# RWKV-7 steps of a two-layer hybrid diffusion backbone: key products, decay preparation and transposes put at other places in the step

## The reference

```python
def step(S, inp):
    r_t, w_t, k_t, v_t, kk_t, a_t = inp
    sa = jnp.einsum('bhij,bhj->bhi', S, kk_t)
    S = (S * w_t[:, :, None, :] - sa[..., None] * (kk_t * a_t)[:, :, None, :]
         + v_t[..., None] * k_t[:, :, None, :])
    return S, jnp.einsum('bhij,bhj->bhi', S, r_t)
```

## Time and profile before

| | |
|---|---|
| runs (3) | median 2116.42 us, 2113.2 to 2116.71 |
| the profiled execution | 2119.79 us, its span 2117.8 us |
| busy share of the span | PE 94%, PEld 87%, DVE 62%, ACT 42%, POOL 36% |
| RWKV steps | about 387 to 553 us (layer 0) and 1425 to 1595 us (layer 1) |
| granted TensorE clock, mean of the span | 0.975 |

### The profile page before, as it was taken

How to read it: one execution, slowest core, us unless ns; L and a number is a source line. 1 busy time by engine, 2 the same in 40 slices (tenths; PEclk the granted TensorE clock), 3 DMA queues, 4 the chain that set the end, 5 groups by cost and what they waited for, 6 DMA issues and landing times.

```text
span 2117.8 us, 47803 instructions
## 1 busy us (share of the span) xinstructions
PE 1980.8 (94%) x20520; PEld 1836.1 (87%) x20520; DVE 1304.2 (62%) x2049; ACT 895.8 (42%) x1701; POOL 769.2 (36%) x603
## 2 busy tenths in 40 slices
PE   6999999888999999999979999988889989999998
PEld 5998866677898999999979987657778989999998
DVE  5755347566679888831239452675566898888112
ACT  4535554333445444531154364544343544445221
POOL 5332244333433434332213321742252334343431
PEclk8999999899999999999989999999999999999999
DMA  8553210000122332344225432000001222232221
GB/s 271 162 169 120 78 19 2 22 28 3 47 77 60 94 86 80 88 140 140 83 90 180 149 109 61 9 22 3 28 25 51 70 77 84 80 91 78 75 80 67
DMA packets 255272, 169.42 MB, mean 80 GB/s; under 512 B 23873, under 2 KB 228223, under 8 KB 255063
## 3 DMA queue, kind: packets, MB, share of 16 engines
q1 hardware_dynamic: 254835, 166.32, 26.1%
q10 hardware_dynamic: 227, 0.07, 0.0%
HBM read 162.21 MB, written 4.15 MB: 79 GB/s over the span
## 4 chain that ended last, share of the span: by engine, by line
PE 77%; DVE 11%; ACT 7%; issue 2%; SPq 1%; POOL 1%; DMA 1%; DVEq 0%; ACTq 0%; POOLq 0%
PE PS L1126 12%; PE PS L1128 12%; PE PS L1127 12%; PE PS L1809 7%; PE PS L1810 7%; PE PS L1811 7%; PE PS L1537 5%; PE PS L1084 2%; ACT arena L2177 1%; SPq L542 1%; PE PS L1559 1%; DVE U_r L3195 1%; DVE U L2806 1%; ACT whi_r L2006 1%; PE PS L1192 1%
## 5 line engine op out<-in xcount | busy, mean ns | idle before, releaser
L781 POOL TENSOR_TENSOR ring_r<-ring,whi_r 128x1024 fp32r<-128x1024 f32 (+1 forms) x128 | 311.3, 2433 | 685.4 <-ACT whi_r L2006 685.4
L1126 PE MATMUL PS<-rwp_r,whi_r 128*128 128x320 f32 x1440 | 455.7, 316 | 12.4 <-DVE arena_r L2468 4.6
L1128 PE MATMUL PS<-rwp_r,ring_r 128*128 128x320 f32 x1440 | 448.0, 311 | 0.0
L1127 PE MATMUL PS<-U_r,whi_r 128*128 128x320 f32 (+1 forms) x1048 | 323.9, 309 | 0.0
L1126 PEld LDWEIGHTS PS<-rwp_r,whi_r 128*128 128x128 f32 x1440 | 273.3, 190 | 26.5 <-issue 19.5
L1127 PE MATMUL PS<-arena_r,whi_r 128*128 128x320 f32 (+1 forms) x904 | 282.3, 312 | 0.0
L1128 PEld LDWEIGHTS PS<-rwp_r,ring_r 128*128 128x128 f32 x1440 | 273.2, 190 | 0.0
L2006 ACT ACTIVATE whi_r<-ring 128x1024 fp32r<-128x1024 f32 (+1 forms) x128 | 131.2, 1027 | 296.1 <-PE PS L1128 295.2
L1127 PEld LDWEIGHTS PS<-U_r,whi_r 128*128 128x128 f32 x1048 | 196.9, 188 | 0.3
L2464 DVE TENSOR_TENSOR arena<-arena 128x640 f32<-128x640 f32 x32 | 61.2, 1912 | 214.8 <-ACT arena L1945 214.4
L1127 PEld LDWEIGHTS PS<-arena_r,whi_r 128*128 128x128 f32 x904 | 172.8, 191 | 0.2
(11 more groups left out here) (506 smaller groups left out, 4956.1 us busy)
## 6 DMA issues: line engine op xcount, KB each, us to landing
ring<-in_ffn_w SPq DMA_DIRECT2D x120, 512.0 KB, 3.8
rwp<-in_ada_w SPq DMA_DIRECT2D x64, 512.0 KB, 4.8
ring<-in_w_in SPq DMA_DIRECT2D x50, 512.0 KB, 4.6
U<-in_ada_w SPq DMA_DIRECT2D x16, 512.0 KB, 9.2
ring<-in_w_out SPq DMA_DIRECT2D x16, 512.0 KB, 3.8
arena<-in_ada_w SPq DMA_DIRECT2D x16, 512.0 KB, 4.6
ring<-in_ffn_w SPq DMA_DIRECT2D x16, 384.0 KB, 3.2
out<-arena SPq DMA_DIRECT2D x5, 512.0 KB, 3.6
```

Source lines behind the costliest of these rows:

```text
L781: g.tensor_tensor(rings_r[:, slot_of[n], 0:size(n), :], slot(n)[:, 0:size(n), :], whis[:, q % 2, 0:size(n), :].bitcast(F32), ALU.subtract) ...
L1126: mm(out, w[0][:, k, :], hi[:, cols], start=start, stop=False)
L1127: mm(out, w[0][:, k, :], lo[:, cols], start=False, stop=False)
L1128: return mm(out, w[1][:, k, :], hi[:, cols], start=False, stop=stop)
```

## The change

Four edits, all inside the RWKV steps. No instruction is added or taken away; five places in the lists and one wait are moved.
- PE: the key products (L1559) stand ahead of the first round of the doubling in steps 1, 3 and 4. Steps 0 and 2 keep the old order.
- PE: the wait for `yr_read` stands ahead of the diagonal products, not ahead of the transposes.
- DVE: `prep_scan(k + 1)` is split by unit. Unit `l` is prepared at the head of level `l`, ahead of its adds; and `adds(2, 3)` stands ahead of the mask of the feature products (L2932).
- ACT: `decays(k + 1)` is split by unit. Unit `l` stands behind the copies of level `l`.

```diff
@@ PE
                             pe.wait_ge(s["rw_keys"], at["rw_keys"] + i + 1)
-                            if k:
-                                pe.wait_ge(s["yr_read"], at["yr_read"] + i - 1)
...
                             pe.wait_ge(s["rw_feat"], at["rw_feat"] + i + 1)
+                            if k:
+                                pe.wait_ge(s["yr_read"], at["yr_read"] + i - 1)
...
+                        if k in (0, 2):
+                            first_round()
+                            key_products()
+                        else:
+                            key_products()
+                            first_round()
@@ ACT
-                        if k < NC - 1:
-                            decays(k + 1)
-                        else:
+                        if k == NC - 1:
                             y_high(range(3, 4))
...
                         for l in range(2):
                             copies(3 + l, 4 + 2 * l)
+                            if k < NC - 1:
+                                decays(k + 1, l)
@@ DVE
                         adds(0, 1)
-                        if k < NC - 1:
-                            prep_scan(k + 1)
-                        else:
+                        if k == NC - 1:
...
                         adds(1, 2)
+                        adds(2, 3)
                         for d in range(2):
...
-                        adds(2, 3)
                         if k == 3:
                             ssd_scaled([3])
                         for l in range(2):
+                            if k < NC - 1:
+                                prep_scan(k + 1, (l,))
                             adds(3 + l, 5 + 2 * l)
```

More of the change, by code:

```diff
@@ L1545, in added, with first_round @@
                             pe.wait_ge(s["inv_add"], at["inv_add"] + 10 * k + 2 * r + d + 1)
[L1547 to L1561, removed]
+                        def first_round():
+                            for d in range(2):
+                                pe.wait_ge(s["rw_q"], at["rw_q"] + 2 * k + d + 1)
+                                each(d, 2, 0, "QT", "Q")
+                                each(d, 2, 256, "Q", "QT").then_inc(s["inv_mm"], 1)
@@ new lines, in key_products @@
+                        def key_products():
+                            for d in range(2):
+                                b, a, i = units[d], 4 * d, 2 * k + d
+                                pe.wait_ge(s["rw_tok"], at["rw_tok"] + 2 * i + 2)
+                                if i == 0:
+                                    pe.wait_ge(s["yn_read"], at["yn_read"] + 1)
+                                if i == 4:
+                                    pe.wait_ge(s["yn_read"], at["yn_read"] + 2)
+                                for hh, (f, q) in enumerate(hq):
+                                    ins = mm(PS[:, a + hh % 2, 256 * f:256 * f + 256],
+                                             b["KB"][q, f, 0, :], b["RK"][k % 2][q, f, :, :], start=True, stop=True)
+                                ins.then_inc(s["rw_prod"], 1)
@@ L2189, in y_high, with decays @@
                             A(rp_r[:, YSEQ[n], :], U[:, YTILES[YSEQ[n]], :], ACT.Copy).then_inc(s["in_hi"], 1)
[L2191 to L2206, removed]
+                    def decays(k, d):
+                        b, i = units[d], 2 * k + d
+                        act.wait_ge(s["rs_dve"], at["rs_dve"] + i + 1)
+                        if k:
+                            act.wait_ge(s["rw_feat"], at["rw_feat"] + i - 1)
+                            act.wait_ge(s["rw_last"], at["rw_last"] + i - 1)
+                            if k > 1:
+                                act.wait_ge(s["sp_ready"], at["sp_ready"] + i - 3)
+                        A(b["e2"], b["c"], ACT.Exp, scale=ISQE)
+                        A(b["e1"], b["c"], ACT.Exp, scale=-ISQE)
+                        A(b["e3"], b["e3"], ACT.Exp, scale=-ISQE)
+                        A(EMID[:, 2 * d:2 * d + 2], MID[:, 2 * d:2 * d + 2], ACT.Exp, scale=-ISQE).then_inc(s["rs_exp"], 1)
+                    for d in range(2):
+                        decays(0, d)
                     for c in range(NC - 2, NC):
@@ L2792, in mlstm_centre, with prep_scan @@
                         dve.wait_ge(s["dve_step"], step())
-                    def prep_scan(k):
-                        for d in range(2):
+                    def prep_scan(k, ds):
+                        for d in ds:
                             b, i = units[d], 2 * k + d
@@ L2836, in _ @@
                         else:
-                            prep_scan(0)
+                            prep_scan(0, range(2))
                         normalise(c)
```

## The result

| | median us | lowest to highest | runs |
|---|---|---|---|
| before | 2115.78 | 2113.2 to 2116.71 | 4 |
| after | 2095.32 | 2092.18 to 2097.18 | 4 |

The ratio is 0.9899, with a 95% interval of 0.9884 to 0.9914: 20.5 us less between the medians. The forecast was 2088.3 us with a range of 2079 to 2101. The profiled execution of after took 2094.3 us, its span 2092.3 us, at a mean granted clock of 0.978.

What follows compares the result with a forecast made beforehand. PE was taken to bound the kernel (77% of the chain), so gains come where it waits. Steps 26.0, contention -2.4 and clock +4.5 gave 28.1 us off 2116.42: 2088.3 us, range 2079 to 2101.

Steps and rivals of the forecast that it cites:

- Key products: PE's list, steps 1, 3 and 4: key products ahead of the first round start the second round 2.0 us earlier.
- Preparation and early sum: DVE, around fourth round and first level: removed waits gain 1.5 + 0.6, less 0.75 given back: 1.35 us a step.
- 0.75 us given back: Second level: unit 0's preparation delays the first level's sum, so PE starts that level 0.7 to 0.75 us later.
- Transposes: Start of steps 2, 3 and 4: no wait for DVE's read, gaining 1.0, 0.35 and 1.0 us.
- ACT's new place: ACT, inside the levels: unit 0's decays take 1.1 us ahead of a copy, hidden by 0.5 us; unit 1's use idle time.
- Step 4: Inside step 4, without preparation: ACT's splits limit the first level's copies to 2.1 us earlier, counted as the whole inside gain.
- Contention in steps 2 and 3: DVE's unit 1 preparation and row scalings beside POOL's keys: 0.6 us lost in each step, 2.4 in two layers.
- Clock: RWKV steps: five low-clock stretches behind PE's removed waits become two, gaining 3 x 1.5 = 4.5 us.
- Its own range: Main case's range, 2080 to 2094 us: one clock stretch more or less, contention from 0 to 4 us.
- Contention at its upper bound: Rival, chance 0.12: DVE beside POOL's keys loses 6.4 us a layer, clock gives only 1.5; time 2101.7 us.

Runs made afterwards that it cites:

- e1: Kernel before with only the key products moved ahead of the first round in steps 1, 3 and 4: 2101.27 us, ratio 0.9930.
- e2: Kernel after with PE's part as before, so only the preparation, decays and adds(2, 3) are moved: 2109.88 us, ratio 0.9968.
- e5: Kernel after with step 4's key products behind the first round again: 2092.05 us, ratio 0.9883.
- e8: Kernel after with unit 0 prepared behind adds(0, 1), unit 1 ahead of the second level's sums, step 2's row scalings put apart: 2091.38 us, ratio 0.9873.
- e3: Kernel before with only the wait for yr_read moved from the transposes to the diagonal products: 2110.82 us, ratio 0.9968.
- e7: Kernel after, with POOL's keys from step 1 on waiting until DVE has prepared both units: 2088.24 us, ratio 0.9870.
- e9: Kernel after with step 4's gating held, POOL's keys held until preparation ends, and unit 0 prepared early: 2077.93 us, ratio 0.9810.
- e11: Kernel before with key products first in steps 1, 3 and 4, and POOL's gating held in step 4: 2095.17 us, ratio 0.9889.
- e10: Kernel before with only POOL's gating in step 4 held until DVE's two products are done: 2113.76 us, ratio 0.9981.
- e6: Kernel after, with POOL's gating in step 4 held until DVE's two products are done: 2088.39 us, ratio 0.9857.

## Why the prediction was right, and where it was not

The time fell within the range, 7.0 us above the forecast: 20.5 us gained where 28.1 were forecast, with a median of before that one more run took from 2116.42 to 2115.78. By its own steps:

- **Key products, 2.0 us in steps 1, 3 and 4**: 2.08 in steps 1 and 3 (e1), 0 in step 4.
- **Preparation and early sum, 1.35 us a step**: 1.48 in step 1 (e2). Step 0 fits: with one low stretch at nearly the same place it has 34.87 us in e1 and 33.65 in e5. The 0.75 us given back in it was over-sized: the new wait is 0.36 us, and e8, which takes it away, gets 0.42.
- **Transposes, 1.0, 0.35 and 1.0 us**: 0.97 into step 4 and 0.42 into step 3 (e3). Into step 2, step 1's 4.51 less 2.08 and 1.48 leaves 0.95.
- **ACT's new place**: hidden, as said: PE's wait for the copy behind it is 0.22 us (0.23 before). Its table load of 1.28 us, which the forecast had not listed, makes the exponentials of step 1 begin 0.6 us after the preparation, and that is hidden too.
- **Step 4, 2.1 us inside it: the step that failed.** "L2921 (2.25 us) stays ahead of `adds(1, 2)`, and ACT's two splits ... hold back the first level's copies: the copies can come 2.1 us earlier and no more, so 2.1 stands for the whole of the step's inside". The limit by ACT was right: with the gating held, the copies start 2.07 us earlier than before and no more. The two other halves were wrong. L2921 did not stay at 2.25 us; it took 4.25, because 2 us earlier it meets POOL's L861, which starts 7.6 us after the first mask before and after alike. And the gain does not pass from the copies to the end of the step: the four low parts, which the sum did not name, stretch from 5.4 to 6.0 us beside POOL's L781 (layer 1), and the last sum starts at 23.3 us, where it started at 23.4 before. The contention was priced for the decay preparation and the row scalings alone, though the products were in the earlier trace rows. Price of the miss: 2.1 us in layer 0, 2.0 in layer 1.
- **Contention in steps 2 and 3, 0.6 us each: mis-sized.** Without it the forecast for the lengths was 1.7 and 3.5 us, and e7 has 33.19 - 31.52 = 1.67 and 33.12 - 29.59 = 3.53. With it, after stands at 0.07 (layer 1: -0.58) and 2.34. So it costs 1.60 and 2.29 us in step 2 and 1.19 in step 3. The scans were right in size (0.73 to 1.75 us for two); the row scalings (1.67 to 2.15) and the small copy (0.17 to 0.52) came on top, and the solve waits for the last of the chain. In steps 0 and 1 it cost nothing, as said (28.80 and 28.79 us with and without).
- **Clock, 4.5 us: wrong in reason, its size not settled.** Of the five low stretches behind step 0's opening one is left, in step 4 of layer 0, where it costs 0.15 us (29.36 against 29.21 in layer 1). The forecast tied them to the waits of 1.4 and 0.6 us. But e1 keeps these and has no low stretch behind the opening, and e3, which keeps them too, has four.
- **Its own range**, 2080 to 2094, is wider than its terms: one stretch (1.5 us) either way and contention from 0 to 4 us give 2084.4 to 2091.4.

In numbers, at the high clock and with 1.35 us for step 0 (taken over from the forecast; no pair of profiles shows step 0 free of the low clock): layer 0 gained 1.35 + 4.51 + 0.07 + 2.34 + 0 = 8.3 us, layer 1 1.35 + 4.41 - 0.58 + 2.35 + 0.11 = 7.6. That is 15.9 against the forecast's 23.6: 4.1 us missing in step 4, 3.8 in steps 2 and 3, 0.2 over in step 1. The two profiled executions differ by 25.5 us. 24.1 of it lie between the first mask of step 0 and the last output of step 4 (168.28 to 157.19 us in layer 0, 169.75 to 156.73 in layer 1), so 8.2 are left for the clock there, against 4.5. But before's execution stood 4.0 us above its median and after's 1.0 below; between the medians it is 20.5, and 4.6 are left. Both are remainders, and so estimates. In the pair of profiles, on which the forecast was built, the clock made up for half of what the steps missed: that is luck.

So the direction and most terms were right, and the time came out 7 us higher because the meetings with POOL, in steps 2 and 3 and in step 4, were priced too low or not at all. The rival "Contention at its upper bound" (2101.7) named the right mechanism for steps 2 and 3, but not step 4, where the larger part of the miss lies.

**Open**: why the low stretches went. Every kernel with the key products first in steps 1 and 3 has at most one behind the opening (e1, e5 to e9, e11 and after), the others up to six (before, e10), four (e3) or one (e2). Stretches also vanish in steps 0 and 2, whose order is unchanged, and each count is from one execution; that is an association, not a cause. Nor is it settled why step 2 lost 0.65 us more in layer 1 than in layer 0; PE's idle time that the profile puts down to issue is 0.9 us there against 0.4.

## What to carry to other kernels

When an edit brings an instruction forward, ask which work of other engines does not come forward with it, and lay both on one time axis; here two products that came 2.07 us earlier took 2.00 us longer, and the low parts that came 0.7 us earlier took 0.6 longer. Follow the gain past the first wait as well: the instruction that set the end of the step stood 10 us behind the one that the edit reached. A part measured alone can lose (e2 in step 3) or give nothing (keys in step 4) and still be worth its whole price once the meeting is taken away, and one wait on the engine that has time to spare was enough for that: where PE waits for VectorE and GpSimd has slack, let GpSimd be late.

## What the runs showed of the hardware

**Two-input products of GpSimd and VectorE shut each other out nearly completely.** Alone the two products take 1.55 us (0.78 each) and the instruction of the gating 2.90 (e6). Started together they take 4.25 and 3.55 us (after; 4.25 and 3.56 in e1). If GpSimd waits for the first product, 0.78 us, and the second product for GpSimd's whole instruction, DVE would need 0.78 + 2.90 + 0.78 = 4.46 us and POOL 3.68: measured are 4.25 and 3.55. The Trainium skill's page "SBUF — State Buffer", section "Who interferes with whom", says that a DVE instruction with two SBUF inputs contends with a GpSimd instruction that reads SBUF, and that the ports that they share are an exclusive lock. This case's runs agree for these pairs, but not for every one: in e5, layer 0, the two products run beside GpSimd's TENSOR_SCALAR (L864, which reads SBUF) and take 1.55 us, as alone. Where both are two-input products, the price is near the length of the instruction that is met, so that long ones (2.9 us here) are dearer neighbours than short ones (0.72 us).

**The small copy L2823, with one input, also took 0.52 instead of 0.17 us** beside POOL's keys, and 0.17 again in e7.

**The activation table load is issued ahead of its wait.** In step 1 it starts at 431.90, before the preparation that its exponentials wait for has ended (432.17 + 0.43 = 432.60), and takes 1.28 us; they begin at 433.20, 0.02 us after its end.
